# A hybrid decoder layer on one core: the order of the first eight attention jobs

## What is computed

```
p_c = masked_softmax(einsum(qg, kc), mask_c)       # compressed keys (63 of them)
o_c = p_c @ vc
s_s = einsum(qg, kg)                                # selected blocks
p_s = masked_softmax(s_s, mask_s); o_s = p_s @ vg   # all keys up to the query block
p_w = masked_softmax(einsum(qg, kw), mask_w)        # a window of 512 keys back
o_w = p_w @ vw
o = gb[0] * o_c + gb[1] * o_s + gb[2] * o_w
```

## Time and profile before

| what | us |
|---|---|
| median of three runs | 1782.23 (1780.85 to 1784.22) |
| the profiled execution | 1778.61 |
| span of its trace | 1776.8 |
| NSA stage on PE, first score to last output | about 150 to 449 |

### The profile page before, as it was taken

How to read it: one execution, slowest core, us unless ns; L and a number is a source line. 1 busy time by engine, 2 the same in 40 slices (tenths; PEclk the granted TensorE clock), 3 DMA queues, 4 the chain that set the end, 5 groups by cost and what they waited for, 6 DMA issues and landing times.

```text
span 1776.8 us, 23287 instructions
## 1 busy us (share of the span) xinstructions
PE 1692.3 (95%) x8496; PEld 1415.4 (80%) x8496; DVE 1236.7 (70%) x1666; ACT 729.8 (41%) x1367; POOL 860.2 (48%) x659
## 2 busy tenths in 40 slices
PE   7998899999999999899999898999999999999997
PEld 6886788877788888788888686877788888877886
DVE  6755578776777777346555635777887887789965
ACT  5104577776223224115332303434444444543444
POOL 3343344443423332230312143459988888689851
PEclk9998999999999999999999999999999999999999
DMA  5230010110110112216201222036444435685332
GB/s 193 79 119 18 25 37 25 37 41 8 48 48 24 60 48 107 72 48 209 80 33 35 90 101 83 24 126 210 147 147 133 161 131 164 217 323 178 118 132 95
DMA packets 80171, 176.47 MB, mean 99 GB/s; under 512 B 7676, under 2 KB 24252, under 8 KB 79936
## 3 DMA queue, kind: packets, MB, share of 16 engines
q1 hardware_dynamic: 67944, 135.71, 23.1%
q10 hardware_dynamic: 12120, 39.34, 5.9%
HBM read 136.21 MB, written 38.81 MB: 99 GB/s over the span
## 4 chain that ended last, share of the span: by engine, by line
PE 56%; DVE 16%; POOL 11%; ACT 8%; issue 7%; DMA 2%; ACTq 0%; SPq 0%; DVEq 0%; POOLq 0%
PE ps L1014 13%; PE ps L1018 13%; PE ps L1017 13%; DVE x_t L2620 4%; PE ps L1193 3%; ACT x_t L1907 2%; POOL sum_s L925 2%; PE ps L1270 2%; POOL w_lo L919 2%; PE ps L1164 2%; DVE x_t L2649 2%; POOL w_lo L975 2%; PE ps L1212 2%; DMA w_raw<-in_w_tiles 2%; PE ps L1213 1%
## 5 line engine op out<-in xcount | busy, mean ns | idle before, releaser
L1014 PE MATMUL ps<-h_hi,w_hi 128*128 128x512 f32 x1108 | 439.9, 397 | 20.1 <-DVE h_lo L2081 5.9
L1017 PE MATMUL ps<-h_lo,w_hi 128*128 128x512 f32 x1108 | 435.8, 393 | 0.0
L1018 PE MATMUL ps<-h_hi,w_lo 128*128 128x512 f32 x1108 | 435.4, 393 | 0.0
L868 POOL TENSOR_TENSOR w_hi<-w_raw,ones 128x1024 fp32r<-128x1024 f32 x55 | 114.4, 2081 | 587.4 <-PE ps L1014 498.4
L1014 PEld LDWEIGHTS ps<-h_hi,w_hi 128*128 128x128 f32 x1108 | 210.5, 190 | 71.7 <-issue 9.2
L1018 PEld LDWEIGHTS ps<-h_hi,w_lo 128*128 128x128 f32 x1108 | 210.5, 190 | 44.8
L1017 PEld LDWEIGHTS ps<-h_lo,w_hi 128*128 128x128 f32 x1108 | 210.8, 190 | 42.6
L896 POOL TENSOR_SCALAR probs<-probs,nsa_inv,gate_sig 128x640 f32<-128x640 f32 (+7 forms) x128 | 100.2, 783 | 172.9 <-DVE nsa_inv L2284 172.9
L2620 DVE SCALAR_TENSOR_TENSOR x_t<-ps,par,x_t 128x1023 f32<-128x1023 f32 x84 | 107.7, 1282 | 79.1 <-ACT x_t L1907 77.6
L871 POOL TENSOR_TENSOR w_lo<-w_raw,w_hi 128x1024 fp32r<-128x1024 f32 x55 | 146.7, 2668 | 4.3
L2080 DVE TENSOR_TENSOR pt_lo<-ps,pt_hi 128x512 fp32r<-128x512 f32 (+1 forms) x148 | 101.7, 688 | 58.1 <-ACT pt_hi L1663 56.2
(11 more groups left out here) (373 smaller groups left out, 4102.4 us busy)
## 6 DMA issues: line engine op xcount, KB each, us to landing
w_raw<-in_w_tiles SPq DMA_DIRECT2D x109, 512.0 KB, 3.5
w_raw<-in_w_tiles SPq DMA_DIRECT2D x55, 256.0 KB, 3.1
s_new<-in_w_tiles SPq DMA_DIRECT2D x44, 256.0 KB, 4.1
z_dram<-x_t ACTq DMA_DIRECT2D x21, 512.0 KB, 2.9
b<-z_dram SPq DMA_DIRECT2D x33, 256.0 KB, 4.2
q_st<-q_dram SPq DMA_DIRECT2D x64, 128.0 KB, 2.8
t_dram<-t_new ACTq DMA_DIRECT2D x22, 256.0 KB, 5.1
s_dram<-s_new SPq DMA_DIRECT2D x22, 256.0 KB, 3.1
```

The costliest lines, as they stand in the source:

```text
L868: pool.tensor_tensor(w_hi[s][:, :], w_raw[s][:, :], ones[:, :].to_broadcast([P, KT * P]), ALU.mult).then_inc(w_hi_made.sem, w_hi_made.up())
L1014: ins = mm(out_ap, whi, x_hi, start=first, stop=False)
L1017: mm(out_ap, whi, x_lo, start=False, stop=False)
L1018: return mm(out_ap, wlo, x_hi, start=False, stop=last)
```

## The change

The pairs of the first group are turned round, so that the long job of each pair comes first. Nothing else is edited; the order of heads and steps, their places in `probs`, the waits and the order of query loads all follow from the list.

```diff
-JOB_BLOCKS = [(0, i) for i in (0, 7, 1, 6, 2, 5, 3, 4)] + [(1, i) for i in (4, 3, 5, 2, 6, 1, 7, 0)]
+JOB_BLOCKS = [(0, i) for i in (7, 0, 6, 1, 5, 2, 4, 3)] + [(1, i) for i in (4, 3, 5, 2, 6, 1, 7, 0)]
```

## The result

The new order is slower: 1785.81 us against 1781.86 (medians of ten runs each). The ratio on record, taken over all these runs, is 1.0029 with a 95% interval of 1.0018 to 1.0040; the two medians alone give 1.0022. The forecast was 1778.8 us and a ratio of 0.998, so the kernel moved the other way. The time lies just inside the range given, which ended at 1786. Of the rivals it is A, the clock. The ten runs of the kernel before reach from 1775.05 to 1784.22, which is more than the 3.4 us that the prediction took from three.

What follows compares the result with a forecast made beforehand. Head-chain latency binds the NSA stage up to 230 us, PE after it. Terms 0 - 2.1 - 1.75 + 0.45 = -3.4 us, carried to the median of 1782.23, give 1778.8 us; 8 in 10 range 1775.5 to 1786.

Steps and rivals of the forecast that it cites:

- Rival A: Clock stays low behind the new gaps; ten us behind each of three gives +6.1 us, 1788.3; chance 0.15.
- three signs: First step of block 1 after 181 us, clock under 0.8 from 165 to 190, or second group not starting earlier.
- Start: First long job, block 7: its first step starts at about 164.75 instead of 175.24, 10.5 us earlier.
- Next twelve entries: From block 7's first step to its last window head: 9.5 us against 10.67 now, head 7 at 174.25.
- The short job in the middle: Block 0's short heads 8 to 15, done at 187.2; the start's 10.5 us given back in full.
- my bound of 14.3: Slower bound for block 0's short heads, at the two-block heads' pace: 14.3 us against 12.95, 1.4 worse.
- The next pair: Blocks 6 and 1, up to head 32: 2.1 us less idling and 1.75 us of clock gained.
- the 1.75 us of clock: Gain from the low-clock stretch behind 192.49 going away: 2.5 + 1.0 us at half speed.
- The rest: Remainder of the first group: -0.85 for a vanished wait, +1.3 for neighbours further apart in size, together +0.45 us.
- the one on the clock: Low clock lasts about 3.7 us behind a gap, and 3.5 us of it behind 192.49 goes.
- the argument that I set against A: In much of the low-clock time behind the new gaps PE waits for others anyway.

## Why the prediction was wrong

By its own steps, walk against trace:

| point | walk | measured |
|---|---|---|
| p0.0 starts | 164.75 | 165.12 |
| head 7 scored | 174.25 | 176.14 |
| p1.0 starts | 179.5 | 182.04 |
| head 15 done (p1.2 starts) | 187.2 | 192.15 |
| head 32 against before | -3.85 | +3.8 |
| head 64 against before | -3.4 | +5.35 |

All three signs that it named for being wrong came: p1.0 at 182.04 and not before 181, a clock of 0.70 from 165 to 190, and the second group later and not earlier.

**Start.** Right, to 0.4 us: the first transposes came 10.1 us earlier. This stretch I had walked at the low clock.

**Next twelve entries** (9.5 us forecast, 11.0 measured). I let the low clock end as soon as behind 175.24 before. It lasted until 171.

**The short job in the middle** (12.95 forecast, 16.0 measured, beyond my bound of 14.3). This is the largest miss. From head 7 to p1.0 it took 5.90 us, walked at 5.25; from p1.0 to the end of head 15 it took 10.1, walked at 7.7, because the clock was at 0.50 from 181 to 195, all through the thin short heads. Filling just this place gave 4.1 us back in the medians.

**The next pair** (3.85 gained forecast, 1.3 measured: 41.8 us from 192.15 to 233.92, against 43.05 before). The wait for block 6 was 2.86, forecast 2.6, and block 6's last part went by without a gap over 1 us, as forecast. PE idled 1.6 us less in this stretch (5.5 against 7.1), forecast 2.1. But the 1.75 us of clock were not gained: the new order had its own low stretches here, up to 195 and from 208 to 215. And 0.9 of the 1.3 is the output and the product that it has yet to do at head 32, so at equal work it gained 0.4.

**The rest** (+0.45 forecast, +1.6 measured): the output and the product that lie behind head 32 now make 0.9 of it; I had left them out of both terms.

The step that failed is the one on the clock: that it would be back about 3.7 us behind a gap, and that the change would take 3.5 us of low clock away. It put 16.3 us more of it there up to head 32 (37.1 against 20.8), or 13.8 more in the whole kernel over all runs. The waits of the chain were about those of the walk.

Rival A had the cause and too high a price. It took half a us for each further us at half clock. That would be 19.8 us further (the 16.3, and the 3.5 that the forecast took away), so -3.4 + 9.9 = +6.5, against +5.35 at head 64. The filled runs and the 86 runs of the kernel before both put the price at about 0.3. So the argument that I set against A, that PE waits for others in much of that time, was true of a part of it, and did not make up for the rest. I gave A 0.15.

The clock is not all of the miss. The terms of the forecast without its 1.75 of clock add up to -1.65, and with the clock filled up the new order is still 1.5 us behind at head 64. The gain of some 3 us that these terms promised is not there at equal clock either, and no run shows which of them it was.

The Trainium skill, "TensorE: Matmul & The Clock Gate", Part 1 ("What's actually happening"), has activity release the throttle; the trace agrees: 24 matmuls of 512 columns at the start of the new order took away most of the 16 us at 0.50 there. By the clock of 0.93 from 149.6 to 175 us in that run, 3.6 us of them are left. The Trainium skill, "TensorE: Matmul & The Clock Gate", "Why this matters for your kernels", asks for matmul bursts without long idle gaps between them. The trace agrees, and shows it for short gaps too: 1.69 and 1.09 us in a row were followed by 14 us at the lower level. It also shows that a gap alone does not decide it: 2.86 us ahead of p4.0 were followed by 7 us at the lower level in the new order, and by none where the short job was filled.

What stays open: why the second group loses 26 us at the longer lag, what sets where a low stretch begins and how long it lasts, and the 0 to 2 us of order at equal clock.

## What to carry to other kernels

When a list of work is reordered and PE is the engine that sets the pace, look at the granted clock of the stretch first: a reorder that adds up to less waiting can still lose if it puts thin work (small heads, few steps) behind the gaps. Price the time at the lower clock from the runs and not as half of it: here it was 0.3 us for each us. Where the clock falls, try to fill the waits with matmuls into a free bank before anything cleverer; here 45 of them gave 0.66% against the same order. The longer lag in the first group gave 0.83%, and turning the pairs round alone cost 0.29%. And an order and its lag are one choice: the order lost at the lag of 2560 and was as good or better at 3584 in the first group.

## What the runs showed of the hardware that was not expected

The granted clock fell to the lower level in the second of two gaps of PE of 1.69 and 1.09 us with 0.5 us of work between them, and stayed there for 14 us while PE was busy for 3.5 to 5.0 us of each 5. Behind the gap ahead of p4.0 (2.86 or 2.87 us) it fell in one execution and did not in two others. Forty-five matmuls of 512 columns in the gaps kept it at 0.95 up to head 32; the same number of 64 columns did not do so reliably (single runs 1775.7 to 1788.2). A us at the lower level cost 0.3 us and not half a us. With the clock at 1.00 through the first stretch, the old order's five runs lay within 3.2 us (1770.2 to 1773.4), against 12.5 us in twelve runs with the thin filling; and over 86 runs of the kernel before, time and low clock go together with a correlation of 0.83. Much of what looks like noise of this kernel is the clock.
